# Chunk recurrence of an RWKV-7 layer: the off-diagonal 128x128 form of N, one product per pair of heads

## The reference, cut to what matters

```python
def wkv7_scan(s0, r, w, k, v, a, b):
    def step(s, inp):
        r_t, w_t, k_t, v_t, a_t, b_t = inp
        sa = jnp.einsum('bhij,bhj->bhi', s, a_t)
        s = s * w_t[:, :, None, :] + sa[..., :, None] * b_t[..., None, :] + v_t[..., :, None] * k_t[..., None, :]
        y = jnp.einsum('bhij,bhj->bhi', s, r_t)
        return s, y
```

## Time and profile before

| | us |
|---|---|
| median of 3 runs | 1236.2 (1234.26 to 1239.66) |
| the profiled execution | 1238.11 |
| its span, first to last instruction | 1236.0 |
| TensorE busy (matmul), share of the span | 1107.1, 90% |
| VectorE / ScalarE / GpSimd busy | 488.7 / 284.7 / 195.6 |
| mean granted TensorE clock | 0.962 |

### The profile page before, as it was taken

How to read it: one execution, slowest core, us unless ns; L and a number is a source line. 1 busy time by engine, 2 the same in 40 slices (tenths; PEclk the granted TensorE clock), 3 DMA queues, 4 the chain that set the end, 5 groups by cost and what they waited for, 6 DMA issues and landing times. The chain is left out here.

```text
span 1236.0 us, 25152 instructions
## 1 busy us (share of the span) xinstructions
PE 1107.1 (90%) x10677; PEld 850.0 (69%) x10677; DVE 488.7 (40%) x1145; ACT 284.7 (23%) x568; POOL 195.6 (16%) x210
## 2 busy tenths in 40 slices
PE   3599999968999998999899999999897899988874
PEld 3488888857888887888777888888355455545441
DVE  3134555555656562455527501100336322211126
ACT  2013232333454453000033401000011111111112
POOL 3000000014444440000000008400000222211110
PEclk9799999988999999999999999999998799998998
DMA  3323212211000000322821123350878699999985
GB/s 103 87 69 80 53 53 53 53 29 46 4 4 4 5 4 16 115 68 77 197 74 55 48 68 85 107 150 1 323 293 309 248 415 414 414 416 418 416 341 207
DMA packets 113838, 182.98 MB, mean 148 GB/s; under 512 B 10364, under 2 KB 88520, under 8 KB 105029
## 3 DMA queue, kind: packets, MB, share of 16 engines
q1 hardware_dynamic: 107190, 168.56, 38.9%
q0 software_dynamic: 5168, 8.56, 1.9%
q10 hardware_dynamic: 1383, 4.42, 0.9%
HBM read 173.24 MB, written 17.55 MB: 154 GB/s over the span
## 5 line engine op out<-in xcount | busy, mean ns | idle before, releaser
L266 PE MATMUL rk_ps<-xT,rk_w 128*128 128x260 f32 x768 | 176.1, 388 | 9.7 <-DMA rk_lw<-in_a_lora_up 9.7
L266 PEld LDWEIGHTS rk_ps<-xT,rk_w 128*128 128x128 f32 x768 | 146.0, 192 | 37.2 <-issue 9.8
L266 PE MATMUL mg_psg<-xT,w_merge 128*128 128x260 f32 x512 | 116.6, 387 | 2.7 <-PEq L110 2.7
L266 PEld LDWEIGHTS mg_psg<-xT,w_merge 128*128 128x128 f32 x512 | 98.3, 192 | 18.0 <-issue 2.7
L2087 DVE SCALAR_TENSOR_TENSOR ex_sg<-tl_psA,ex_slot_rs,ex_sg 128x128 f32<-128x128 f32 x32 | 11.2, 351 | 140.6 <-ACT ex_sg L1887 140.4
L266 PE MATMUL uv_psu<-xT,w_uv 128*128 128x260 f32 x256 | 59.2, 391 | 3.0 <-ACTq L1041 3.0
L266 PE MATMUL mg_psp<-ya,w_merge 128*128 128x260 f32 x256 | 57.6, 383 | 0.0
L266 PE MATMUL psv<-xT,w_uv 128*128 128x260 f32 x256 | 57.5, 383 | 0.0
L266 PE MATMUL mg_psp<-r_all,w_merge 128*128 128x260 f32 x256 | 57.4, 382 | 0.0
L266 PEld LDWEIGHTS uv_psu<-xT,w_uv 128*128 128x128 f32 x256 | 49.2, 195 | 11.0 <-ACTq L1041 3.3
L684 PE MATMUL ck_b<-ck_X,ck_V 64*64 64x64 f32 x1280 | 51.6, 223 | 4.8 <-issue 3.9
(11 more groups left out here) (469 smaller groups left out, 2009.4 us busy)
## 6 DMA issues: line engine op xcount, KB each, us to landing
wd<-in_moe_w_down SPq DMA_DIRECT2D x15, 1024.0 KB, 25.3
rk_w<-in_w_in SPq DMA_DIRECT2D x24, 512.0 KB, 5.2
tl_x<-in_moe_w_down SPq DMA_DIRECT2D x9, 1024.0 KB
w_uv<-in_w_in SPq DMA_DIRECT2D x16, 512.0 KB, 5.1
w_merge<-in_w_in SPq DMA_DIRECT2D x16, 512.0 KB, 4.5
xT<-in_moe_w_gate SPq DMA_DIRECT2D x5, 1024.0 KB
xT<-in_moe_w_up SPq DMA_DIRECT2D x5, 1024.0 KB
bonus_all<-in_moe_w_gate SPq DMA_DIRECT2D x5, 1024.0 KB, 21.4
```

Source lines behind the costliest of these rows:

```text
L266: last = eng.matmul(out[:, h, 0:TH], weights[:, k, :], xT[:, k, h * TH:(h + 1) * TH], start=(k == 0), stop=(k == NK - 1))
```

## The change

N moves into a tile `ck_N` of 128x128 for each pair of heads, in its two off-diagonal blocks: the N of `lo` in rows 0 to 63, columns 64 to 127, that of `hi` in the other. The diagonal blocks stay zero. Then

- W of levels 1 to 4 is one product for a pair, 128 rows and 128 columns stationary, 64 columns moving, in place of two of 64x64. Level 0 keeps the 64x64 form.
- `scores` makes one product for a head, with all 128 columns of bk as the stationary operand (64 rows) and 128 columns moving, in place of two with 64 columns each. `lo` heads land in bank 0, `hi` heads in bank 1.
- N leaves PSUM by a predicated copy over a tile that holds zeros and the diagonal of ones from the start (`strict`), so GpSimd's addition of the diagonal is gone, and `ck_mb` and `ck_nb` with it. X comes from `ck_N` in two half instructions (`first_x`). Both other parts of a bank are masked by VectorE in two instructions (`rest`): 64 partitions into `ck_L`, 128 partitions into `by_r`.
- the output product of `new_state` runs over 128 rows, the r-part of `old_state` over 64 instead of 128.
- TensorE takes `turn_x` and `turn_bk_v` of a group together, ScalarE follows, and VectorE's queue at the chunk's end is reordered.
- before the loop GpSimd clears `ck_N` and writes the diagonals.

```diff
             def scores(c, g):
...
                     for rows, which in ((lo, 0), (hi, 1)):
-                        eng.matmul(b4(b[0])[rows, n, :], bk[rows, p, rows], L[rows, p, which, :], start=True, stop=True)
-                    for rows, others, which in ((lo, hi, 0), (hi, lo, 1)):
-                        last = eng.matmul(b4(b[1])[others, n, :], bk[rows, p, others], L[rows, p, which, :],
-                                          start=True, stop=True)
+                        last = eng.matmul(b4(b[which])[:, n, :], bk[rows, p, :], L[rows, p, which, :], start=True, stop=True)
...
             def turn_x(c, g):
-                eng.wait_ge(s_x1[g], c + 1)
-                eng.wait_ge(s_mb[g], c + 1)
+                eng.wait_ge(s_x1[g], c * 2 + 2)
+                eng.wait_ge(s_b0[g], c * 2 + 2)
...
             def level(c, lv):
...
-                    for n, p, own, other in heads(g):
-                        last = eng.matmul(b64(bank[g][1])[other if lv else own, n, :], nb[own, p, :], Z[own, p, :],
-                                          start=True, stop=True)
+                    if lv == 0:
+                        for n, p, own, other in heads(g):
+                            last = eng.matmul(b64(bank[g][1])[own, n, :], N[own, p, other], Z[own, p, :], start=True, stop=True)
+                    else:
+                        for n in range(GP):
+                            p = g * GP + n
+                            last = eng.matmul(b64(bank[g][1])[:, n, :], N[:, p, :], Z[:, p, :], start=True, stop=True)
...
             def old_state(c, g):
...
-                    eng.matmul(b64(b[0], GP * HD)[lo, n, :], wv[:, p, 0, :], L[:, p, 0, CH:P], start=True, stop=True)
+                    eng.matmul(b64(b[0], GP * HD)[lo, n, :], wv[lo, p, 0, :], L[lo, p, 0, CH:P], start=True, stop=True)
...
             def new_state(c, g):
...
-                    eng.matmul(b64(b[3])[lo, n, :], wv[lo, p, 0, :], mb[lo, p, CH:P], start=True, stop=True)
+                    eng.matmul(b64(b[3])[lo, n, :], wv[:, p, 0, :], by_r[c % 2][:, p, 0, :], start=True, stop=True)
...
                 for g in range(G):
                     turn_x(c, g)
-                for g in range(G):
                     turn_bk_v(c, g)
...
         @block.vector
-            def masked_n(c, g):
+            def strict(c, g):
+
                 eng.wait_ge(s_eo[g], c + 1)
-                eng.tensor_tensor(mbs[c % 2][:, grp(g), :], b4(bank[g][0]),
-                                  m.causal[:, :].unsqueeze(1).to_broadcast([P, GP, P]), ALU.mult).then_inc(s_mb[g], 1)
-
-            def masked_k(c, g, rows, which):
-                mask = m.causal[:, :].unsqueeze(1).to_broadcast([P, GP, P])
+                for own, other, which in ((lo, hi, 0), (hi, lo, 1)):
+                    eng.copy_predicated(N[own, grp(g), other],
+                                        m.causal[own, 0:CH].bitcast(I32).unsqueeze(1).to_broadcast([HD, GP, CH]),
+                                        b4(bank[g][which])[own, :, 0:CH]).then_inc(s_n[g], 1)
+
+            def rest(c, g, which):
+
                 eng.wait_ge(s_eo[g], c + 1)
-                eng.tensor_tensor(L[rows, grp(g), which, :], b4(bank[g][1])[rows], mask[rows], ALU.mult).then_inc(s_lk[g], 1)
+                other = hi if which == 0 else lo
+                done = s_b0 if which == 0 else s_b1
+                scores = b4(bank[g][which])
+                eng.tensor_tensor(L[other, grp(g), which, 0:CH], scores[other, :, 0:CH],
+                                  m.causal[other, 0:CH].unsqueeze(1).to_broadcast([HD, GP, CH]), ALU.mult).then_inc(done[g], 1)
+                eng.tensor_tensor(by_r[c % 2][:, grp(g), which, :], scores[:, :, CH:P],
+                                  m.causal[:, CH:P].unsqueeze(1).to_broadcast([P, GP, CH]), ALU.mult).then_inc(done[g], 1)
...
         @block.gpsimd
-            def with_diagonal(c, g):
-
-                eng.wait_ge(s_mb[g], c + 1)
-                eng.tensor_tensor(nb[:, grp(g), :], mbs[c % 2][:, grp(g), 0:CH],
-                                  m.ident2[:, :].unsqueeze(1).to_broadcast([P, GP, CH]), ALU.add).then_inc(s_nb[g], 1)
-                eng.wait_ge(s_nb[g], c + 1)
+            def first_x(c, g):
+
+                eng.wait_ge(s_n[g], c * 2 + 2)
                 if c:
                     eng.wait_ge(s_u[g], c)
-                eng.tensor_tensor(X[:, grp(g), :], nb[:, grp(g), :],
-                                  m.levels[:, 0, :].unsqueeze(1).to_broadcast([P, GP, CH]), ALU.mult).then_inc(s_x1[g], 1)
+                for own, other in ((lo, hi), (hi, lo)):
+                    eng.tensor_tensor(X[own, grp(g), :], N[own, grp(g), other],
+                                      m.levels[own, 0, :].unsqueeze(1).to_broadcast([HD, GP, CH]), ALU.mult).then_inc(s_x1[g], 1)
...
+            eng.memset(N[:, :, :], 0.0).then_inc(s_zero, 1)
+            eng.wait_ge(s_zero, 3)
+            for own, other in ((lo, hi), (hi, lo)):
+                eng.tensor_copy(N[own, :, other], m.ident2[own, :].unsqueeze(1).to_broadcast([HD, NP, CH])).then_inc(s_zero, 1)
```

More of the change, by code:

```diff
@@ L552, in phase_chunks @@
         wv = sb("ck_wv", [P, NP, 2, HD])
-        mbs = [sb(f"ck_mb{n}", [P, NP, P]) for n in range(2)]
-        nb = sb("ck_nb", [P, NP, CH])
+        by_r = [sb(f"ck_by_r{n}", [P, NP, 2, CH]) for n in range(2)]
+        N = sb("ck_N", [P, NP, P])
         X = sb("ck_X", [P, NP, CH])
@@ L697, in old_state @@
                     p = g * GP + n
-                    eng.matmul(b64(b[0], GP * HD)[lo, n, :], wv[:, p, 0, :], L[:, p, 0, CH:P], start=True, stop=True)
-                    last = eng.matmul(b64(b[0], GP * HD)[hi, n, :], wv[:, p, 1, :], L[:, p, 1, CH:P], start=True, stop=True)
+                    eng.matmul(b64(b[0], GP * HD)[lo, n, :], wv[lo, p, 0, :], L[lo, p, 0, CH:P], start=True, stop=True)
+                    last = eng.matmul(b64(b[0], GP * HD)[hi, n, :], wv[hi, p, 1, :], L[hi, p, 1, CH:P], start=True, stop=True)
                 last.then_inc(s_rhs[g], 1)
@@ L716, in new_state @@
                 last.then_inc(s_s[g], 1)
-                mb = mbs[c % 2]
                 for n in range(GP):
                     p = g * GP + n
-                    eng.matmul(b64(b[3])[lo, n, :], wv[lo, p, 0, :], mb[lo, p, CH:P], start=True, stop=True)
-                    last = eng.matmul(b64(b[3])[hi, n, :], wv[hi, p, 1, :], mb[hi, p, CH:P], start=True, stop=True)
+                    eng.matmul(b64(b[3])[lo, n, :], wv[:, p, 0, :], by_r[c % 2][:, p, 0, :], start=True, stop=True)
+                    last = eng.matmul(b64(b[3])[hi, n, :], wv[:, p, 1, :], by_r[c % 2][:, p, 1, :], start=True, stop=True)
                 last.then_inc(s_y[g], 1)
@@ L786, in _ @@
                 for g in range(G):
+                    b = bank[g]
                     eng.wait_ge(s_zt[g], c + 1)
-                    eng.activation(Z[:, grp(g), :], b64(bank[g][0]), ACT.Copy).then_inc(s_z1[g], 1)
-                for g in range(G):
+                    eng.activation(Z[:, grp(g), :], b64(b[0]), ACT.Copy).then_inc(s_z1[g], 1)
                     if c:
@@ L793, in _ @@
                         eng.activation(wv[lo, grp(g), 0, :], st[lo, grp(g), :], ACT.Copy).then_inc(s_s0[g], 1)
-                for g in range(G):
-                    b = bank[g]
                     eng.wait_ge(s_tb[g], c + 1)
@@ L859, in _ @@
                 r_rows(eng, 0, rows, which)
+            eng.wait_ge(s_zero, 5)
             for g in range(G):
-                masked_n(0, g)
+                strict(0, g)
             for g in range(G):
-                masked_k(0, g, hi, 0)
-                masked_k(0, g, lo, 1)
-            eng.wait_ge(s_zero, 2)
+                rest(0, g, 0)
+                rest(0, g, 1)
             for c in range(NC):
@@ L885, in _ @@
                 if c + 1 < NC:
-                    masked_n(c + 1, 0)
-                    masked_k(c + 1, 0, hi, 0)
+                    strict(c + 1, 0)
+                    rest(c + 1, 0, 0)
                 for g in range(G):
@@ L932, in _ @@
                 for g in range(G):
[L933 to L934 removed]
+                    first_x(c + 1, g)
+                eng.wait_ge(s_x1[1], c * 2 + 4)
                 for g in range(G):
```

24 lines of the change are left out of this document (11 added, 13 removed).

## The result

| | before | after |
|---|---|---|
| median, us | 1235.5 (1234.26 to 1239.66, 4 runs) | 1261.1 (1260.19 to 1262.14, 4 runs) |
| ratio | | 1.0201 (95%: 1.0175 to 1.0228) |
| the profiled execution, span | 1236.0 | 1260.4 |
| TensorE busy (matmul) | 1107.1 | 1133.4 |
| chunk loop, from the first turn of X to the last y | 196.4 | 220.8 |

The account below looks back on a forecast made before the run. TensorE's queue of full-width W weight loads was to bind the levels, VectorE and TensorE the boundary. 19.2 + 8.4 + 0.8 - 0.7 = +27.7 us on the median 1236.2 gave 1264 us, range 1246 to 1284.

Parts of the forecast that it names:

- the pace of a 128*128 record: W bursts of levels 1 to 4: records start 0.111 us apart, set by the full-width weight load.
- levels and `old_state`: Chunk loop: longer W bursts add 0.53 us a level, three more form changes in `old_state` 0.3; together +19.2 us.
- pauses: TensorE's pauses without a cause in the profile: 13% fewer matmul records, so -0.7 us, bounds 0 and -3.
- boundary: Between chunks: twelve smaller VectorE masks and TensorE's wait for y, +1.2 us at 7 boundaries, +8.4 us.
- scores: Score bursts: half the records at twice the width balance, 0 us, bounds +-0.4 us a burst.
- before the first chunk: GpSimd's clear and diagonals put 2.5 us ahead of its rows of bk: +0.8 us, bounds 0 and 2.4.
- The predicted 0.3 behind it: At each boundary, TensorE's stall for y of the new state: 0.3 of the 1.2 us.
- C: Slow predicated copy (first part, 1272) or 64*128 scores of two heads not overlapping (second, 1270); both 1278; chance 0.15.
- A: TensorE bursts cost by instruction count: 1232.7, the same (0.05), or with cheap masks and hidden stall 1226, faster (0.05).
- B: Copies hold the levels, so the longer W is hidden: 1248 (1252 with the prediction's masks); chance 0.13.
- a clock below 1.00 in the loop: Chunk loop: granted clock under full, listed as a sign of being wrong; no term contained it.
- The dearer sum of 1270: Chunk loop: full array drains at about ten more mode changes a chunk, 0.07 each, 5.6 us in all, giving 1270.

Follow-up runs that it names:

- e4: The changed kernel with each head's scores again as two products with 64 stationary columns each: 1262.8 us, ratio 1.0208.
- e8: The changed kernel with 16 small products, whose output nobody reads, added behind g1's W burst in levels 1 to 4: 1284.9 us, ratio 1.0384.
- e5_deferred: The changed kernel with four r-masks a chunk moved from VectorE's queue at the boundary into levels 0 and 1: 1259.4 us, ratio 1.0155.
- e2: The kernel before with only the 128x128 W of levels 1 to 4 added, `ck_N` filled by GpSimd copies: 1254.5 us, ratio 1.0119.

## Why the prediction was right, and where its terms were off

The forecast was 1264 us (1246 to 1284), slower with 0.88; it came out at 1261.1. The difference of 25.6 stands against a sum of 27.7. The main mechanism, the pace of a 128*128 record, is right and shown. That the sum lies within 2 us is luck: the price of undisturbed levels was too low by 9 to 10 us, the pauses that went were priced some 7 too low, and the boundary 3 to 4 too high. By its terms:

| term | predicted, us | measured in the loop |
|---|---|---|
| levels and `old_state` | +19.2 | mean to mean +2.56 a chunk, x8 = +20.5 |
| pauses | -0.7 (0 to -3) | -7.5 (8.4 to 0.9), most of it contained in the line above, some in the line below |
| boundary | +8.4 | +0.57 x7 = +4.0 (undisturbed +0.73, 5.1) |
| scores | 0 | in the burst +0.03 x8 = +0.2; in front of it 0.2 a chunk (e4), contained in the levels |
| clock | none | +1.3 in the last chunk, not in the means |
| before the first chunk | +0.8 | +2.3 |
| phases behind the loop | 0 | -2.3, scatter |

By chunks the loop's 24.4 us are 1.3 in chunk 0, where before the turn of g1 waited 0.73 for GpSimd, 18.5 in chunks 1 to 6 and 4.6 in the last, with its half clock; so the lines above, scaled up from chunks 1 to 6, give 26.0.

**W and the levels: right in mechanism, and its size was hit by two errors.** The pace of 0.111 from the router's weight loads was measured as 0.111; g1's burst starts 0.94 after g0's (0.9 predicted). The first half is 1.93 (1.88), the second 1.30 instead of 1.25, the level 3.23 (3.12). But the step that compared with the mean of 2.59 compared with levels that held pauses. Undisturbed, a level before takes 2.47 and level 4 2.25, so the change adds 3.7 us a chunk by these least values, 28 to 29 in all and not 19, of which about 1 a chunk came back because the pauses went. The prediction took the pauses as a small share by record count (13% fewer, -0.7), and read only the largest line of them, 3.9 of 8.4 us. That term is off by ten and outside its own bounds: e8 shows that the pauses do not go with the count of the records.

**The boundary: right in kind, twice too large.** VectorE's work grew by 0.63 (0.90 predicted; neighbours overlap, most starts lie 0.34 to 0.45 apart). TensorE does wait for y, 0.78 and 0.44. The predicted 0.3 behind it came as 0.11 of idle time: VectorE's queue and TensorE's turns now end within 0.16 of each other, TensorE's last. TensorE's own boundary is 0.73 longer where no pause disturbs it, 1.2 predicted. The masks ahead of y count in it: e5_deferred took four away and won 1.24. The predicated copy at 0.44 against 0.42 was a fair guess; the first part of C is out, and e4 puts the second at 0.2 us a chunk, in front of the burst and not in it.

**Before the first chunk: too small by 1.5.** GpSimd at the start of the changed kernel:

```profile
275.63 0.95 POOL L919 MEMSET ck_N<- 128x1024 f32 x1
276.64 1.70 POOL L922 COPY ck_N<-ident 64x512 f32<-64x512 f32 x2
278.39 1.62 POOL L617 TENSOR_TENSOR ck_bk<-br_all,ck_pi 64x512 f32<-64x512 f32 x1
279.98 1.71 POOL L618 TENSOR_TENSOR ck_bk<-k_all,ck_pi 64x512 f32<-64x512 f32 x1
```

The clear and the diagonals cost what was taken (0.95 and 0.85 each), and b and k end at 281.69, 0.6 later than worked out. What was left out is most likely the wait `PE psv L640 <- DVE ck_by_r L840` of 1.0 above (no run tests it): the masks of the first chunk have no boundary in front of them but the first turn waits for them as well. Masks were counted 7 times where 8 count. The start itself lay at 285.83 to 288.79 in the eight kernels that share it, so of these 2.3 us one or so is chance.

**The rivals.** A (count of instructions) would have needed bursts of 0.7 us; they are 1.06 to 1.10. B (the longer W hidden) falls with the first half of 1.93 and with e2 alone at +16. One sign that the prediction named as wrong did come, a clock below 1.00 in the loop, with 1.3 us. As to the modes of the array: the last 128*128 record of a W burst starts at 414.69 and ends at 414.96, the first 64*64 one starts at 414.89; before the change the step from the last W record to the first X product was as long, 0.20 us (390.30 to 390.50), but there V of g0 ended only at 390.35, so it is no price without a change. The Trainium skill, page "TensorEngine Tiling (Array Packing)", section "Key Properties", has the array drained at a change of mode. The trace agrees in part: the next mode starts 0.07 before the last record ends, here and in front of the changed kernel's scores, but not before that record has started, while the 64*64 scores of e4 start among the last X records, and that difference is worth 0.2 us. The dearer sum of 1270 was not reached, though with terms that cancel this settles little. `old_state` with its three more changes costs 0.1 (e1 against before, 4.70 and 4.59) to 0.4 (after against e2, 5.69 and 5.25), predicted 0.3.

## What to carry to other kernels

Price a TensorE burst by what each record loads and where it lies in the array: in these bursts a 64*64 record cost 0.031 us, with two tiles side by side, and a 128*128 record 0.111 to 0.119, with 36 moving columns and with 64 alike. So a block matrix that is half zeros halved the instructions and lengthened the burst from 0.68 to 1.10 us. When the length of a stage is read as a mean, look for undisturbed ones first; a mean may hold pauses that the change removes or brings back. Add up all lines of such pauses, not the largest one. And when masks are cut into smaller pieces, count them at every place where someone waits for them, the first pass included.
